# Retention's output product as seven half-size products in a stage of its own

## The reference, cut to what matters

```python
q, k, v, g, xr, gr, m_ret, m_rnn = jnp.split(rms_norm(x) @ w_in, ...)
o = head_norm(retention(rotary(q), rotary(k), v))       # 4 heads, chunks of 128 tokens
y_ret = (silu(g) * o) @ w_ret_o                         # (1024 x 2048) @ (2048 x 1024)
y_rnn = (rg_lru(conv(xr)) * gelu(gr)) @ w_rnn_o         # (1024 x 1024) @ (1024 x 1024)
x = x + (sigmoid(m_ret) * y_ret + sigmoid(m_rnn) * y_rnn) @ w_out
x = x + (silu(gate) * val) @ w_down                     # the ConvFFN
# retention, for a head and a chunk i of 128 tokens (decays left out):
#   o_i   = (q_i k_i^T, masked) v_i + q_i state
#   state = state * decay + k_i^T v_i
```

## Time and profile before

| | us |
|---|---|
| median of three runs | 2010.44 |
| the profiled execution: its own time | 2009.94 |
| its span in the profile | 2008.2 |
| PE busy | 1983.1 (99%) |
| PE weight loads busy | 1656.7 (82%) |
| DVE busy | 1382.1 (69%) |
| ACT busy | 908.8 (45%) |
| POOL busy | 243.0 (12%) |

### The profile page before, as it was taken

One profiled execution on the slowest core, in us unless ns is written; L12 is line 12 of the kernel. 1 busy time (PEld: TensorE's weight loads), 2 busy tenths in 40 slices (PEclk: granted clock), 3 DMA queues, 4 the chain that ended last, 5 costly groups with the idle time before them and its releaser, 6 DMA issues.

```text
span 2008.2 us, 25125 instructions
## 1 busy us (share of the span) xinstructions
PE 1983.1 (99%) x9304; PEld 1656.7 (82%) x9304; DVE 1382.1 (69%) x1659; ACT 908.8 (45%) x1155; POOL 243.0 (12%) x190
## 2 busy tenths in 40 slices
PE   8999999999999999999999999999999999999998
PEld 6888888888888888887888888998788888888887
DVE  7877777776654444614876776747988788776766
ACT  6433344343445555413454543345644544543335
POOL 2000000000000000011355554200000000000000
PEclk9999999999999999999999999999999999999999
DMA  6343454454554343455333234731222222156533
GB/s 257 127 156 127 157 188 145 157 188 146 188 178 168 136 157 126 147 169 172 119 116 122 78 120 151 252 127 63 98 83 91 70 76 104 63 187 231 203 101 132
DMA packets 185637, 285.10 MB, mean 142 GB/s; under 512 B 9825, under 2 KB 123873, under 8 KB 185313
## 3 DMA queue, kind: packets, MB, share of 16 engines
q1 hardware_dynamic: 165264, 206.62, 31.0%
q0 software_dynamic: 20304, 77.60, 9.9%
HBM read 200.29 MB, written 83.89 MB: 142 GB/s over the span
## 4 chain that ended last, share of the span: by engine, by line
PE 88%; DVE 8%; ACT 2%; issue 1%; DMA 1%; SPq 0%; DVEq 0%; ACTq 0%
PE ps L330 29%; PE ps L332 29%; PE ps L331 29%; DVE ws L313 1%; PE ps L1138 1%; DVE wx L2018 0%; DMA qkv<-scr_v 0%; ACT ri L1539 0%; DVE th L2196 0%; DVE ri L2207 0%; DVE th L2200 0%; DVE ri L2201 0%; DVE gel L2210 0%; DVE th L2208 0%; PE ps L1089 0%
## 5 line engine op out<-in xcount | busy, mean ns | idle before, releaser
L1392 ACT ACTIVATE wx<-raw 128x1024 fp32r<-128x1024 f32 (+1 forms) x152 | 137.3, 905 | 249.4 <-DVE raw L1994 128.8
L330 PE MATMUL ps<-xs,wx 128*128 128x512 f32 x612 | 239.0, 391 | 2.1 <-DVE xs L2432 1.6
L331 PE MATMUL ps<-xs,wx 128*128 128x512 f32 x612 | 238.2, 389 | 0.0
L332 PE MATMUL ps<-xs,wx 128*128 128x512 f32 x612 | 238.1, 389 | 0.0
L2018 DVE TENSOR_TENSOR wx<-raw,wx 128x1024 fp32r<-128x1024 f32 (+1 forms) x152 | 156.1, 1028 | 30.4 <-ACT wx L1392 30.0
L330 PE MATMUL ps<-sc,wx 128*128 128x512 f32 x448 | 174.3, 389 | 0.0
L331 PE MATMUL ps<-sc,wx 128*128 128x512 f32 x448 | 174.3, 389 | 0.0
L332 PE MATMUL ps<-sc,wx 128*128 128x512 f32 x448 | 174.3, 389 | 0.0
L1427 ACT ACTIVATE ub<-ps 128x512 f32<-128x512 f32 x112 | 66.9, 597 | 161.7 <-PE ps L332 159.1
L330 PEld LDWEIGHTS ps<-xs,wx 128*128 128x128 f32 x612 | 114.9, 188 | 28.4 <-issue 2.7
L332 PEld LDWEIGHTS ps<-xs,wx 128*128 128x128 f32 x612 | 114.9, 188 | 24.0
(11 more groups left out here) (283 smaller groups left out, 4762.7 us busy)
## 6 DMA issues: line engine op xcount, KB each, us to landing
raw<-w_in SPq DMA_DIRECT2D x80, 512.0 KB, 5.4
scr<-ost POOLq DMA_DIRECT2D x32, 1024.0 KB, 5.3
raw<-w_up SPq DMA_DIRECT2D x44, 512.0 KB, 3.9
tq<-w_down SPq DMA_DIRECT2D x88, 128.0 KB, 3.0
scr_t<-tq POOLq DMA_DIRECT2D x22, 512.0 KB, 3.2
scr_h<-vt POOLq DMA_DIRECT2D x11, 1024.0 KB, 4.3
scr_v<-ost POOLq DMA_DIRECT2D x8, 1024.0 KB, 4.6
qkv<-scr SPq DMA_DIRECT2D x64, 128.0 KB, 3.1
```

The source lines that it names most:

```text
L330: pe.matmul(out, w(HI), x(HI), start=first, stop=False, skip_group_check=True)
L331: pe.matmul(out, w(HI), x(LO), start=False, stop=False, skip_group_check=True)
L332: return pe.matmul(out, w(LO), x(HI), start=False, stop=last, skip_group_check=True)
L1392: act.activation(dst, src, ACT.Copy).then_inc(sem["f_hi"], 1)
```

## The change

- `reto` leaves retention's steps. Retention's gated output goes from SBUF to DRAM (`scr_yg`, one 256 KB store for each step, on SP) and comes back as four quarter blocks of 1024 features by 512 tokens (tiles `yq`).
- After the 32 steps stands a stage of its own: seven half-size products p, each in four chunks of 24 matmuls, 28 chunks i. For each chunk ACT and DVE split 128x1024 of weights and 128x1024 of y, in two alternating buffer sets; DVE adds the sums of y (`reto_sum`) and of results (`reto_add`, `reto_last`), ACT copies results out (`reto_copy`).
- The sums of w_ret_o's quarter blocks are made by POOL during the last four blocks of the input projection (16 pieces, three subtractions or additions and one store each), in staging tile `tr`; w_down's 22 pieces move up to blocks 0 to 23. The reload of the parked operand (`scr_a`) moves behind them.
- All 128 units of `y_rnn` are dealt out, four to a step, in front of `update`. The split of the next block's weights is done in halves behind the state in steps j = 3 and j = 5 of heads 0 to 2, on ACT and DVE.
- The loops of retention are written out; `state_lo` of the first head goes from DVE to POOL; mixing runs in another order, beside the last chunks.

```diff
-W_AT = [0, 2, 4, 6] + list(range(8, 26))
+W_AT = [0, 2, 4, 5, 6, 7] + list(range(8, 24))
...
+            def reto_combine(j):
+                pool.wait_ge(*late_count(f"tr_in{v}", 64 * (j // 4 + 1)))
+                pool.tensor_tensor(tr[:, v, 0:2, :], tr[:, v, 0:2, :], tr[:, v, 1:3, :], ALU.subtract)
...
+                pool.tensor_tensor(tr[:, v, 2, :], tr[:, v, 0, :], tr[:, v, 2, :], ALU.add)
...
+                pool.tensor_tensor(tr[:, v, 3, :], tr[:, v, 3, :], tr[:, v, 2, :], ALU.subtract)
...
             for b in range(IN_BLOCKS):
                 if b in W_AT:
                     store_tq(W_AT.index(b))
+                if b >= R_BLOCK:
+                    for j in range(4 * (b - R_BLOCK), 4 * (b - R_BLOCK + 1)):
+                        reto_combine(j)
                 store(*in_pair(b), rows(IN_COL[b]))
...
@@ PE @@
+            for r in range(32):
+                scores(r)
+                if r >= 2:
+                    turn_out(r - 2)
+                if r:
+                    outs(r - 1)
+                for unit in range(4 * r, 4 * r + 4):
+                    rnno_unit(unit)
+                if r % 8 < 7:
+                    update(r)
+            turn_out(30)
+            outs(31)
...
+            reto(0, (0, 1, 3))
+            turn_out(31)
+            reto(0, (2,))
+            for i in range(1, R_CHUNKS - 1):
+                reto(i, (0, 1, 3, 2))
+            reto(R_CHUNKS - 1, (0, 1, 2, 3))
...
@@ ACT, at the end of a step @@
                 if j < 7:
+                    act.wait_ge(sem["t_done"], h * 7 + j + 1)
+                    act.activation(state_s[:, slot, HI, :, :], state[:, :, :], ACT.Copy)
+                if j == 3 and h < 3:
...
+                    act.activation(ws[:, s_, HI, 0:BE // 2], raw[:, s_, 0:BE // 2], ACT.Copy)
+                if j == 5 and h < 3:
...
+                    act.activation(ws[:, s_, HI, BE // 2:], raw[:, s_, BE // 2:], ACT.Copy)
...
@@ DVE, in a step, behind sc, gate(r - 2), ktm and scs @@
+                if r >= 2 and r % 2 == 0:
+                    rnno_gated(r // 2 - 1)
+                if r:
+                    stats(r - 1)
+                    coefficients(r - 1)
                 if j < 7:
...
+                if j in (3, 5) and h < 3:
+                    if j == 3:
+                        dve.wait_ge(*late_count("w_hi_a", h + 1))
+                    else:
+                        dve.wait_ge(w_hi[s_], rnno_pair(h + 1)[0] + 1)
+                    last = dve.tensor_tensor(ws[:, s_, LO, part], raw[:, s_, part], ws[:, s_, HI, part].bitcast(F32), ALU.subtract)
...
@@ DVE, behind the steps @@
+            reto_w_lo(0)
+            reto_y_lo(0)
+            rnno_gated(15)
+            gate(30)
+            reto_w_lo(1)
+            reto_y_lo(1)
+            stats(31)
+            coefficients(31)
+            gate(31)
```

More of the change, by code:

```diff
@@ L617, in _, with chunk_load @@
                 sp_.dma_start(stg[:, t % 2, :], scr_y[t * P:(t + 1) * P, :]).then_inc(sem[f"ys_in{t % 2}"], 16)
[L618 to L623, removed]
-            tokens = scr_v.rearrange("(c p) n -> p c n", p=P)
[L627 to L630, removed]
+            tokens = scr_v.rearrange("(c p) n -> p c n", p=P)
+            def chunk_load(r):
+                h, j = STEPS[r]
+                slot = r % 2
+                if r == 0:
+                    sp_.wait_ge(sem["job"], jobs_before(LAST_PAIR) + 5)
+                if r >= 2:
                     sp_.wait_ge(sem["qsp"], r - 1)
@@ L671, in _ @@
[L671 to L684, removed]
@@ L1139, in turn_out @@
                 last.then_inc(sem["ont_ps"], 1)
-            def step(h, j):
-                first = isinstance(h, int)
-                scores(h, j)
-                if not (first and j < 2):
-                    turn_out(*previous(h, j, 2))
-                if not (first and j == 0):
-                    outs(*previous(h, j))
-                if j < 7:
-                    update(h, j)
-                if first and j < EARLY:
-                    last_rnno(j)
-                for n in [] if first and j < 5 else reto_parts(h, j):
-                    reto(*n)
@@ L1615, in step @@
+            act.wait_ge(stored[1], LAST_PAIR * 16)
+            for job in range(2):
+                evac_job(LAST_PAIR, 1, job, ACT.Sigmoid, 8)
+            for r in range(2):
+                qk_hi(r)
+                v_hi(r)
+            for job in range(2, 4):
+                evac_job(LAST_PAIR, 1, job, ACT.Sigmoid, 8)
+            for r in range(32):
+                h, j = STEPS[r]
+                slot = r % 2
                 act.wait_ge(sem["kt_ps"], r + 1)
[L1616 removed]
+                act.activation(ktm[:, slot, HI, :], ps[:, 1, 0:QK], ACT.Copy).then_inc(sem["km_hi"], 1)
@@ L2310, in step, with reto_y_lo @@
+            def reto_y_lo(i):
+                p, c, k = reto_at(i)
+                u, q = i % 2, (0, 1, 1, 0, 2, 1, 0)[p]
+                dve.wait_ge(*late_count("ry_hi", i + 1))
+                dve.tensor_tensor(ysr[u][:, LO, :, :], yq[q][:, k, :], ysr[u][:, HI, :, :].bitcast(F32),
+                                  ALU.subtract).then_inc(late_sem("ry_lo"), 1)
+            for r in range(32):
+                h, j = STEPS[r]
+                slot = r % 2
                 dve.wait_ge(sem["sc_ps"], r + 1)
-                if not (first and j < 2):
+                if r >= 2:
@@ L2348, in step @@
                     else:
-                        last = dve.tensor_copy(stt[:, :, :], ps[:, 3:5, :])
+                        last = dve.tensor_copy(state[:, :, :], ps[:, 3:5, :])
                     last.then_inc(sem["t_done"], 1)
-                for n in parts[:1]:
-                    accumulate(*n)
-                if (j == 3 and not first) or j == 5:
-                    split_lo(dve, h + PAIR_RETO, 0 if j == 3 else 1)
-                if first and j == 2:
-                    split_lo(dve, PAIR_RETO, 0)
@@ new lines, in reto_add @@
+            def reto_add(p, half, n):
+                dve.wait_ge(*late_count("r_b", 4 * p + 4))
+                dve.wait_ge(sem["r_cp"], 8)
+                cols = slice(half * HALF, (half + 1) * HALF)
+                for q in range(2):
+                    t, bank = slice(4 * n + 2 * q, 4 * n + 2 * q + 2), D_BANK[p] + 2 * q
+                    dve.tensor_tensor(yacc[:, t, cols], yacc[:, t, cols], ps[:, bank:bank + 2, :], ALU.add
+                                      ).then_inc(sem["acc"], 1)
@@ L2407, in _ @@
+            mixed_lo(11)
+            for n in range(13, 16):
                 mixed(n)
```

836 lines of the change are left out of this document (461 added, 375 removed).

## The result

The changed kernel takes 2018.73 us, the median of 6 runs (2014.71 to 2020.55); the kernel before, timed beside it, 2010.13 (2009.31 to 2010.77). The ratio is 1.0041, with a 95% interval of 1.0030 to 1.0051: slower by 0.4%. The forecast was no change at 2010.4 us. The time lies in the stated range of 1993 to 2022 us and outside the forecast's own of 2003 to 2018, and it moved where no change was forecast. The profiled execution of the changed kernel took 2020.55 us, 10.6 more than that of the one before.

What follows compares the result with a forecast made beforehand. PE, busy 99% of the span, was taken to bound the kernel. Stretch work 379.2 for 401.0 us and idle 35.0 for 13.2 keep it at 414.2, so the median is 2010.4 us; range 1993 to 2022, the forecast's own 2003 to 2018.

Steps and rivals of the forecast that it cites:

- product stage: Last five chunks and first w_out split: some 27 us DVE work, 5 us POOL holds, against 27.2; 3.5 us idle (0 to 10).
- start: Start of the chunk steps: y_rnn's first unit, scores(2) and turn_out(0) wait after late chunk loads; 1.9 us (0 to 5).
- weight splits: Behind steps 3 and 5 of three heads: DVE's half split, held by POOL, delays update and turn_out; six by 2.75, 16.5 us.
- The work removed: Seven half products for eight: 672 matmuls for 768, 96 x 0.2267 us, 21.8 us less PE work.
- The hold of DVE by POOL: In the steps, two-SBUF-input DVE instructions and POOL reading SBUF exclude each other; otherwise the forecast falls some 14 us to 1996.
- Rival A: The splits hide: DVE's half split finds a gap and six times 2.75 us go; 1993.9 us, chance 0.30.
- Short and even steps: Heads' second chunks and ends, and even steps without a split: late scores and normalised output idle PE 7.2 us.
- End of the steps: Last two steps' outputs: turn_out(30) waits 1.85 us and turn_out(31) 1.5 us, 3.35 us in all.
- Input blocks and the reloaded operand: Input blocks 24 to 27 with POOL's 16 combinations, and the parked operand's later reload: 0 us (reload bounds 0 and 8).
- Rival C: POOL holds DVE in the input blocks: 1.6 us a block, 6 in all; 2017 us, chance 0.08.
- rival B: The clock: split steps idle PE twice within 5 us, six drops of the granted clock; 2020.0 us, chance 0.13.
- Rival D: Product stage chunks bound by preparation, 6.0 us instead of 5.44, 28 chunks costing 15 us; 2026 us, chance 0.06.

Runs made afterwards that it cites:

- eighth kernel: Changed kernel with the edits of experiment 1, experiment 2, experiment 6 and experiment 4 together; 1986.01 us, ratio to the kernel before 0.9875.
- experiment 1: Changed kernel with ACT's hi part of the half weight splits (j = 3 and 5) ahead of the state's hi part; 2003.17 us, ratio to before 0.9965.
- experiment 3: Changed kernel with POOL's mixing multiplication by sigmoid(m_ret) made on one column of 512; 2010.59 us, ratio to before 1.0001.
- experiment 4: Changed kernel with the state's lo part moved from POOL to DVE, behind the previous step's coefficients; 2005.84 us, ratio to before 0.9979.
- experiment 2: Changed kernel with ACT evacuating LAST_PAIR's last two jobs before chunk 1's hi copies; 2015.81 us, ratio to before 1.0026.
- experiment 6: Changed kernel with ACT's mixed hi parts mostly one chunk later and DVE's mixed(4) and mixed_lo(3) before chunk 25's additions; 2012.74 us, ratio to before 1.0012.

## Why the prediction was wrong, point by point

Two steps of the prediction failed. The product stage was priced as a budget of busy time, 3.5 us, where the handing over between ACT and DVE in a fixed order, with POOL's holds in it, cost 9.7; and the sum had no term for the clock, which took 2.9 us in the stretch and 1.6 behind it. The start, 1.9 us for 3.3, is the third and smallest. The prediction's mechanisms of matmuls, weight splits and POOL's holds were borne out. The points in turn:

*The work removed*, 21.8 us: right. 96 matmuls went, and the eighth kernel, whose time beyond the matmuls' own in the stretch is about what it was before (11.9 us against 13.3), is 24.3 us faster.

*The hold of DVE by POOL*, on which the forecast rested: right, shown by experiments 1, 3 and 4: the held operations fall to their undisturbed length when POOL's work comes later, is left out or is moved. The rule of the Trainium skill, "SBUF — State Buffer", section "Who interferes with whom", that the two exclude each other where DVE has two SBUF inputs and GpSimd reads SBUF, agrees with these numbers: 1.43 us against 0.28 for scs, 2.58 against 1.22 for the split, and no difference for the addition out of a PSUM bank.

*Weight splits*, 16.5 us: right in place and mechanism. `update` waited 1.46 to 1.51 us beyond its time in five steps (forecast 1.6) and 0.85 in one, `turn_out` 0.9 in all six (forecast 1.1), 13.7 us in all. Removing their cause gave 15.6. Rival A, that the splits hide, fell.

*Short and even steps*, 7.2 us: too low, and hidden by the splits, which were put too high. The region's total of 24.9 against 23.7 leaves 11.2 us for them. The parts differ too: `turn_out`, forecast 4.8, waited 2.3 us outside the split steps, and the scores, forecast 2.4, waited 5.6, up to 1.5 at once, mostly for POOL's lo parts of q and k. With both of POOL's jobs no longer in one queue, in the eighth kernel, these waits of the scores are gone but for 0.6 us. *End of the steps*: 3.36 us of waits (1.53 and 1.83) against 3.35.

*Input blocks and the reloaded operand*, 0: right. Rival C had no place: PE is not idle once between 500 and 640.

*Start*, 1.9 us: mis-sized, 3.3 and 1.5 of clock. The step had "six DMAs and 3.9 us to landing bring chunk 1 at some 854.5". The v load was issued at 851.7 and landed at 856.8, 5.1 us, while the stg load issued 0.5 us later was in flight too, until 860.2. So the load was 2.3 us late: 1.2 since it took 5.1 us for 3.9, and 1.1 since the six issues began at 849.29, not at 848.1. The 3.9 were the median where the DMAs moved 112 GB/s; here they moved 276 between 854 and 858. ACT's evacuation stood behind the load in order, which experiment 2 confirms.

*Product stage*, 3.5 us: the largest miss, 9.7 with the refill and 1.4 of clock. The prediction summed DVE's work and POOL's multiplications over the last five chunks against PE's time for them, as one budget (and its own figures, 27 and 5 us against 27.2, make 4.8). But ACT and DVE hand one another work in a fixed order there. The largest wait, at 1255.13, is chunk 25's (counted from 0): w_hi(25) on ACT, at 1251.01, stands behind mixed_hi(3), that behind mixed(3), and that on DVE behind mixed(2) and mixed_lo(1), each held by POOL to 1.78 us for 0.69. The split on DVE, w_lo(25), is then held once more, to 1.75 for 1.23. Chunk 26 waits 1.0 us at 1263.01, behind mixed(4), which stands behind two additions out of the banks; this is the place where 2.3 us stayed in experiment 3. At chunk 27, 1270.49, the split of y is held to 2.29 us for 1.22. The last wait, 2.3 us at 1278.34, is for the split of w_out's weights, whose hi part stands behind mixed_hi(7). The timeline of the changed kernel at its waits of 1255.13 and 1270.49:

```profile
1245.20 3.51 POOL L973 TENSOR_TENSOR msg<-msg,yacc 128x512 f32<-128x512 f32 x2 [8.71 <-DMA mrb<-scr_r]
...
1247.49 1.78 DVE L2482 TENSOR_TENSOR mix<-mxf,mix 128x512 fp32r<-128x512 f32 x1
...
1250.10 0.64 ACT L1759 ACTIVATE mix<-mxf 128x512 fp32r<-128x512 f32 x1 [1.87 <-DVE mxf L2476]
...
1251.49 1.28 POOL L973 TENSOR_TENSOR msg<-msg,yacc 128x512 f32<-128x512 f32 x1 [2.77 <-DMA mrb<-scr_r]
...
1252.11 1.75 DVE L2386 TENSOR_TENSOR wsr<-raw,wsr 128x1024 fp32r<-128x1024 f32 x1 [1.44 <-ACT wsr L1686]
...
1255.13 0.77 PE L346 MATMUL ps<-ysr,wsr 128*128 128x512 f32 x1 [3.05 <-DVE ysr L2393]
...
1267.04 2.22 POOL L973 TENSOR_TENSOR msg<-msg,yacc 128x512 f32<-128x512 f32 x1 [1.03 <-DMA mrb<-scr_r]
...
1268.05 2.29 DVE L2393 TENSOR_TENSOR ysr<-yq,ysr 128x1024 fp32r<-128x1024 f32 x1
...
1270.49 0.47 PE L346 MATMUL ps<-ysr,wsr 128*128 128x512 f32 x1 [1.78 <-DVE ysr L2393]
```

*The clock*: rival B had the mechanism and the wrong place. It put six drops into the split steps, which idle 1.5 and 0.9 us within 4 us; none came there. Three came, at waits of 2.5, 3.2 and 2.3 us that the sum had too small, and took 1.5, 1.4 and 1.6 us. Of the 9.2 us by which the balance was short, 2.9 are the clock inside the stretch; a third drop lies outside it. That three drops decide for a slower kernel was the prediction's own condition, and it was met, though at other places than rival B gave.

Rival D, a stage bound by its preparation throughout: no. Up to 1250 it lost 1.0 us in some 24 chunks.

## What to carry to other kernels

A stage in which two engines hand work to each other in a fixed order is not priced by adding up each one's busy time: follow the ring instruction by instruction, and put each hold where it falls. An operation's mean duration can be time in which it is held, so compare it with the same shape elsewhere before calling its engine busy; here more work on DVE made it faster. And where a change leaves PE's waits longer than those that the trace has, the sum needs a term for the clock at each.

## What the runs showed of the hardware

In the profiles of the changed kernel and the eight experiments, the granted clock fell to its lower level fourteen times between 500 us and PE's last matmul, each time at a wait of PE that was 2.1 us or longer beyond the matmul's own time (2.14, 2.15, 2.29, 2.32, 2.38, 2.52, 2.55, 2.67, 2.98 and five of 3.2 to 4.4). In seven of these it fell before the wait's end, in the others at the end or within 1.2 us behind it. At none of those up to 2.06 did it fall. In the kernel before, two waits of 0.94 and 1.09 us beyond the matmul's own time (0.78 and 0.93 of idle time), ending within 2.1 us, were enough; the second is

```profile
923.23 0.63 PE L330 MATMUL ps<-qkvs,ktm 128*128 128x512 f32 x1 [0.93 <-DVE ktm L2319]
```

In the split steps 1.5 and 0.9 us within 4 us were not. So the length of one wait does not decide alone; what does was not tried further.

The run-to-run spread differed between the kernels: 5.8 us over the 6 runs of the changed one (mean granted clock 0.996 to 0.999), 10 runs of experiment 6 over 9.3 us, but 1.1 us over the eighth kernel's 4. Drops that come in one execution and not in the next would do that. The start shows as much across kernels: the edits of experiments 1, 3, 4 and 6 leave it as it is in the changed kernel, and the wait there was 2.5 us in the changed kernel's profiled execution and 3.0, 2.6, 2.7 and 1.3 in theirs, with a drop in all but the last. It was not shown run by run.
